# Both down projections as seven block products instead of eight

## The reference, cut to what matters

```python
# block 1 (D_FF = 2816)
h = rmsnorm(x, norm_ffn[layer])
x = x + (jax.nn.silu(h @ w_gate[layer]) * (h @ w_up[layer])) @ w_down[layer]
# block 2 (D_FF_2 = 4096)
h = _rmsnorm(x, mlp_norm_w[layer])
x = x + jnp.square(jax.nn.relu(h @ w_up[layer])) @ w_down[layer]
```

## Time and profile before

| | us |
|---|---|
| median of 3 runs (lowest to highest) | 3092.11 (3091.37 to 3097.47) |
| the profiled execution, first to last instruction | 3087.7 |
| TensorE busy | 2937.6 (95%) |
| VectorE busy | 1751.3 (57%) |
| ScalarE busy | 1204.6 (39%) |
| GpSimd busy | 1203.0 (39%) |
| mean granted TensorE clock | 0.986 |

### The profile page before, as it was taken

How to read it: one execution, slowest core, us unless ns; L and a number is a source line. 1 busy time by engine, 2 the same in 40 slices (tenths; PEclk the granted TensorE clock), 3 DMA queues, 4 the chain that set the end, 5 groups by cost and what they waited for, 6 DMA issues and landing times. The chain is left out here.

```text
span 3087.7 us, 36537 instructions
## 1 busy us (share of the span) xinstructions
PE 2937.6 (95%) x13886; PEld 2267.0 (73%) x13886; DVE 1751.3 (57%) x2645; ACT 1204.6 (39%) x1806; POOL 1203.0 (39%) x686
## 2 busy tenths in 40 slices
PE   7888998999999999999999899998999999999999
PEld 5656666666788788887887666656778788878887
DVE  5777775875232644445467555577552544455554
ACT  4445553555433433333124344456562322221110
POOL 5322334222244887774124101031103887722221
PEclk9999998999999999999999999999999999999999
DMA  7311212111251223334231311010003233342222
GB/s 199 71 49 48 62 49 55 42 56 55 85 188 48 68 83 86 84 86 137 67 102 43 114 34 38 17 41 18 11 4 109 83 109 109 109 163 95 95 75 75
DMA packets 279422, 236.36 MB, mean 77 GB/s; under 512 B 23860, under 2 KB 252084, under 8 KB 278708
## 3 DMA queue, kind: packets, MB, share of 16 engines
q1 hardware_dynamic: 279288, 234.65, 25.5%
HBM read 171.14 MB, written 53.51 MB: 73 GB/s over the span
## 5 line engine op out<-in xcount | busy, mean ns | idle before, releaser
L952 PE MATMUL big<-g_hi,w_hi 128*128 128x512 f32 x2112 | 688.5, 407 | 32.0 <-POOL w_lo L2458 6.7
L2458 POOL TENSOR_TENSOR w_lo<-w_raw,w_hi 128x1024 fp32r<-128x1024 f32 (+2 forms) x147 | 340.7, 2318 | 919.1 <-ACT w_hi L1375 919.1
L952 PE MATMUL big<-g_lo,w_hi 128*128 128x512 f32 x2112 | 660.0, 394 | 0.0
L952 PE MATMUL big<-g_hi,w_lo 128*128 128x512 f32 x2112 | 658.4, 393 | 0.0
L952 PEld LDWEIGHTS big<-g_hi,w_hi 128*128 128x128 f32 x2112 | 377.8, 190 | 191.2 <-issue 112.7
L952 PEld LDWEIGHTS big<-g_hi,w_lo 128*128 128x128 f32 x2112 | 399.7, 189 | 87.8
L952 PEld LDWEIGHTS big<-g_lo,w_hi 128*128 128x128 f32 x2112 | 398.9, 189 | 86.8
L1375 ACT ACTIVATE w_hi<-w_raw 128x1024 fp32r<-128x1024 f32 (+2 forms) x147 | 146.2, 995 | 417.1 <-PE big L952 402.7
L1403 ACT ACTIVATE a_hi<-a_raw 128x512 fp32r<-128x512 f32 x114 | 72.1, 632 | 332.9 <-POOL a_raw L2465 329.9
L1223 PE MATMUL big<-b_hi,a_hi 128*128 128x512 f32 x456 | 178.7, 392 | 7.9 <-DVE b_lo L2254 6.0
L1223 PE MATMUL big<-b_lo,a_hi 128*128 128x512 f32 x456 | 178.1, 391 | 0.0
(11 more groups left out here) (345 smaller groups left out, 5439.9 us busy)
## 6 DMA issues: line engine op xcount, KB each, us to landing
a_spill<-c SPq DMA_DIRECT2D x54, 512.0 KB, 3.4
g_lo<-a_spill SPq DMA_DIRECT2D x54, 512.0 KB, 5.1
w_raw<-in_w_in SPq DMA_DIRECT2D x51, 512.0 KB, 4.2
w_raw<-in_w_down SPq DMA_DIRECT2D x40, 512.0 KB, 4.3
w_raw<-in_w_up SPq DMA_DIRECT2D x27, 512.0 KB, 6.0
u_raw<-in_w_up SPq DMA_DIRECT2D x27, 512.0 KB, 5.9
rot<-rope_in SPq DMA_DIRECT2D x68, 128.0 KB, 2.3
g_spill<-gst_b SPq DMA_DIRECT2D x16, 512.0 KB, 3.0
```

Source lines behind the costliest of these rows:

```text
L952: ins = pe.matmul(out[0:m, HALF * h:HALF * h + HALF], w[slot][:, col:col + m], x[:, HALF * h:HALF * h + HALF], start=p == 0, stop=p == tot ...
L2458: pool.tensor_tensor(w_lo[s][:, 0:n], w_raw[s][:, 0:n], w_hi[s][:, 0:n].bitcast(F32), ALU.subtract).then_inc(*s_wlo.mark(w))
```

## The change

The down stage now uses the scheme of the up stage. The contraction runs over sets of two chunks (11 sets in mlp1, 16 in mlp2), the output over four jobs of two rows of `xres` each. For each set and job there are seven products of 3 matmuls instead of eight. The activation blocks of a set (two as they are, five differences and copies, 7 x 512 columns) are made in the up stage by VectorE (`even_difference`, `odd_differences`), stored in DRAM (`op_spill`) and come back set by set into four buffers. The weight sums are made by GpSimd (`down_weights`), from raw weights in stretches of one to three sets.

A window is a job with a stretch of sets: the seven products run over the stretch in PSUM, one bank each, and then VectorE adds every product into all the places of the rows where it belongs. There are 18 windows in mlp1, their widths in sets being 1 1 2 3 3 3 3 3 3 3 3 3 3 3 1 1 3 2, and 24 in mlp2: 1 1 2 3, then sixteen of 3, then 1 2 3 3. Two sets of four banks alternate. The norm factor moves into `form`. In mlp2 the square is now an instruction of its own on ScalarE (`square_act`). The job's stores are now of both tiles and the differences, and the next copy into `c1` still waits for the last of them (in mlp1 only every second time).

A cut of the diff:

```diff
--- before.py
+++ after.py
...
+    JOBS, WIDE = 4, 3
+    FINISH = {"mlp1": (0, 3, 1, 2), "mlp2": (2, 1, 0, 3)}
+    PARTS = [(0, 2), (2, 4), (4, 7)]
...
+    BANK_OF = (0, 1, 3, 0, 1, 2, 3)
+    ADDED_BEFORE = {3: 0, 4: 1, 6: 2}
+    ALSO = {0: 3, 1: 4, 2: 6}
+    BANK_FREE = {0: 3, 1: 4, 2: 6, 5: 5}
...
+    def windows(stage):
+
+        since, out = [0] * JOBS, []
+        for t in range(n_sets(stage)):
+            last = t == n_sets(stage) - 1
+            for job in FINISH[stage] if last else [job for job in (0, 3, 1, 2) if job % 3 == t % 3]:
+                out.append((job, since[job], t + 1, t))
+                since[job] = t + 1
+        return out
+
...
+    def bank_set(stage, i):
+
+        n = len(windows(stage))
+        if i < n - 2:
+            return i % 2
+        return n - 1 - i if stage == "mlp1" else 1
...
+                def down_product(i, pos):
+
+                    _, s0, s1, _ = plan[i]
+                    slot, g = d_slot(stage, i, pos), part_of(pos)
+                    out, n, at_set = bank_tiles[bank_set(stage, i)][BANK_OF[pos]], pos - PARTS[g][0], s1 - 1
+                    pe.wait_ge(*s_dlo.at(stage, i, pos))
+                    pe.wait_ge(*s_setl.at(stage, at_set, g))
+                    if pos in ADDED_BEFORE:
+                        pe.wait_ge(*s_drd.at(stage, i, ADDED_BEFORE[pos]))
+                    elif bank_before(stage, i) is not None:
+                        pe.wait_ge(*s_drd.at(stage, bank_before(stage, i), BANK_FREE[pos]))
+                    elif bank_set(stage, i):
+                        pe.wait_ge(*s_dr.at(stage, NJ - 1, "c21"))
+                    elif pos < 2:
+                        pe.wait_ge(*s_ar.at(stage, NJ - 1, pos))
+                    else:
+                        pe.wait_ge(*s_dr.at(stage, NJ - 1, "p3" if pos == 2 else "c11"))
+                    for k in range(s1 - s0):
+                        b = (s0 + k) % 4
+                        for z, (w, x) in enumerate(((d_hi, set_h), (d_hi, set_l), (d_lo, set_h))):
+                            ins = pe.matmul(out, w[slot][:, k, :], x[b][g][:, n, :], start=k == 0 and z == 0,
+                                            stop=k == s1 - s0 - 1 and z == 2)
+                    ins.then_inc(*s_dp.mark(stage, i, pos))
...
+                def square_act(m, r):
+
+                    act.wait_ge(*s_fn.at(stage, m, r))
+                    act.activation(crow[r][:, :], crow[r][:, :], ACT.Square).then_inc(*s_si.mark(stage, m, r))
...
+                    act.activation(set_h[b][g][:, :, :], set_z[b][g][:, :, :], ACT.Copy).then_inc(*s_seth.mark(stage, at_set, g))
...
+                        if not one:
+                            square_act(m - 1, 1)
...
+                        act.wait_ge(*s_fn.at(stage, m - 1, 1))
+                        if not one or m % 2 == 0:
+                            act.wait_ge(*s_asp[(m - 1) % 2].at(stage, m - 1))
...
+                    if not one:
+                        ins = dve.scalar_tensor_tensor(out=c, in0=c, scalar=0.0, in1=r_rep[:, :], op0=ALU.max, op1=ALU.mult)
+                    elif r == 0:
+                        ins = dve.tensor_tensor(c, c, r_rep[:, :], ALU.mult)
+                    else:
+                        dve.tensor_tensor(c, c, r_rep[:, :], ALU.mult).then_inc(*s_fn.mark(stage, m, "scaled"))
+                        dve.wait_ge(*s_fn.at(stage, m, "scaled"))
...
+                def even_difference(m, row):
+
+                    dve.wait_ge(*(s_fn.at(stage, m, 1) if one else s_si.at(stage, m, 0)))
+                    differ(row[:, HALF:T], row[:, HALF:T], row[:, 0:HALF], m, "even")
+
+                def odd_differences(m, even_row, t24_, t3):
+
+                    dve.wait_ge(*(s_fn.at(stage, m, 1) if one else s_si.at(stage, m, 1)))
+                    dve.wait_ge(*s_tf.at(stage, m - 1 if one else m, "even"))
+                    differ(t24_[:, 0:HALF], crow[1][:, HALF:T], even_row[:, HALF:T], m, "t2")
+                    dve.wait_ge(*s_tf.at(stage, m, "t2"))
+                    differ(t24_[:, HALF:T], crow[1][:, 0:HALF], t24_[:, 0:HALF], m, "t4")
+                    differ(t3, even_row[:, 0:HALF], t24_[:, 0:HALF], m, "odd")
...
-                        form(m, 0)
+                    form(m, 0)
                     if final:
-                        for k in range(2, 4):
-                            act_lo(0, k)
+                        for g in range(3):
+                            set_lo(0, g)
+                    if not one:
+                        even_difference(m, crow[0])
                     add(m, "u3", c21, c21, 6, at_("p3"))
...
+                for i, (job, s0, s1, t) in enumerate(plan):
+                    ra, rb = job_rows(stage, job)
+                    u, z = d_u[job][:, :], xres[:, rb, HALF:T]
+                    dest = [u, z, z, xres[:, ra, 0:HALF], xres[:, ra, HALF:T], u, xres[:, rb, 0:HALF]]
...
+                    for pos in range(7):
+                        dve.wait_ge(*s_dp.at(stage, i, pos))
+                        if pos in (2, 5, 6):
+                            dve.wait_ge(*s_drd.at(stage, i, {2: 1, 5: 0, 6: 2}[pos]))
+                        if pos == 0 and s0 == 0:
+                            dve.tensor_copy(dest[pos], banks_[BANK_OF[pos]]).then_inc(*s_drd.mark(stage, i, pos, "first"))
+                        else:
+                            dve.tensor_tensor(dest[pos], dest[pos], banks_[BANK_OF[pos]], ALU.add).then_inc(
...
+                        if pos in ALSO:
+                            both = dest[ALSO[pos]]
+                            dve.tensor_tensor(both, both, banks_[BANK_OF[pos]], ALU.add).then_inc(*s_drd.mark(stage, i, pos))
...
+                        if loading is not None and pos in (3, 4, 5):
+                            set_lo(loading, pos - 3)
+                        if one and leaving and pos in (2, 6):
+                            exit_row(job_rows(stage, plan[i - 1][0])[pos // 6])
+                        if ends_job(stage, i) and pos == 5:
+                            dve.wait_ge(*s_drd.at(stage, i, 5))
+                            dve.tensor_tensor(dest[4], dest[4], u, ALU.add).then_inc(*s_rel.mark(stage, ra))
+                            dve.tensor_tensor(z, z, u, ALU.add).then_inc(*s_du.mark(stage, job))
+                        if ends_job(stage, i) and pos == 6:
+                            dve.wait_ge(*s_drd.at(stage, i, 6))
+                            dve.tensor_tensor(dest[6], dest[6], u, ALU.add).then_inc(*s_rel.mark(stage, rb))
...
+                def down_weights(i, leaving_row=None):
+
+                    n = plan[i][2] - plan[i][1]
+                    block = lambda q: d_block(i, n, q)
+                    sums = lambda pos: d_sum[d_slot(stage, i, pos)][:, 0:n, :]
+                    down_sum(i, 1, block("A21"), block(A22), ALU.add, s_draw[i % 2].at(stage, i), *d_slot_free(stage, i, 1))
+                    down_sum(i, 5, sums(1), block(A11), ALU.subtract, s_dsum.at(stage, i, 1), *([s_dlo.at(stage, i - 1, 5)] if i else []))
+                    down_lo(i, 0)
+                    down_lo(i, 1, s_dsum.at(stage, i, 5))
+                    down_sum(i, 2, block("A21"), block(A11), ALU.subtract, *d_slot_free(stage, i, 2))
+                    down_lo(i, 2, s_dsum.at(stage, i, 2))
+                    down_lo(i, 3)
+                    if leaving_row is not None:
+                        add_squares("final", leaving_row)
+                    down_sum(i, 4, block(A12), d_s2[:, 0:n, :], ALU.subtract, *d_slot_free(stage, i, 4))
+                    down_lo(i, 4, s_dsum.at(stage, i, 4))
+                    down_lo(i, 5)
+                    down_lo(i, 6)
...
+                    out, done = op_spill[n // 2 if one else n], s_asp[n % 2]
+                    last = n == NJ - 1
+                    t24 = end_t24 if last else op_t24[stage]
+                    if not one:
+                        sp.wait_ge(*s_tf.at(stage, n, "even"))
+                        sp.dma_start(out[:, 0:2 * HALF], crow[0][:, :]).then_inc(*done.mark(stage, n, by=16))
...
+                    sp.wait_ge(*s_tf.at(stage, n, "odd"))
+                    t3 = crow[0] if one else (end_t3 if last else op_even[stage])
+                    sp.dma_start(out[:, 2 * HALF:3 * HALF], t3[:, 0:HALF]).then_inc(*done.mark(stage, n, by=16))
+                    sp.dma_start(out[:, 5 * HALF:7 * HALF], t24[:, :]).then_inc(*done.mark(stage, n, by=16))
...
```

More of the change, by code:

```diff
@@ new lines, in _emit, with d_slot_free, ends_job @@
+    D_ORDER = (A11, S1, S3, A12, S4, S2, A22)
+    LAST_ACT = 5
+    def d_slot_free(stage, i, pos):
+        NJ = n_jobs(stage)
+        if i == 0:
+            done = s_st.base(stage) + 7 * (NJ - 1)
+            return [s_al.at(stage, NJ - 1, S3)] if pos == 4 else [(s_st.sem, done + max(pos, 4))]
+        late = [s_tf.at(stage, "end"), s_asp[(NJ - 1) % 2].at(stage, NJ - 1)] if first_late(stage, i, pos) else []
+        return [s_dp.at(stage, i - 1, pos)] + late
+    def ends_job(stage, i):
```

(47 more changed lines are left out.)

682 lines of the change are left out of this document (239 added, 443 removed).

## The result

The changed kernel takes 3140.64 us (median of four, 3135.22 to 3142.37) where the kernel before takes 3091.74 (3085.65 to 3097.47): 1.0155 of it, 95% interval 1.0138 to 1.0172, so 1.6% slower. I had said 3128, in 3060 to 3160, and slower with 0.61. The profiled execution has a span of 3138.8 us against 3087.7.

The account below looks back on a forecast made before the run. TensorE was taken to bound the kernel at 0.2267 us a matmul. Terms -73.4 + 10.7 + 65.7 + 25.1 + 7.5 = +35.6 us took the span from 3087.7 to 3123.3, the median to 3128, range 3060 to 3160 (forecast's own 3100 to 3160).

Parts of the forecast that it names:

- mlp2's up stage, +65.7: From mlp2's up stage into its down stage's start: a 23.1 us loop replaces TensorE's 19.04 per job, costing +65.7 us.
- The turns: VectorE and GpSimd alternate on SBUF while GpSimd has work queued; in mlp2's up-stage loop 4.6 to 5.8 us, mean 5.2.
- my 17.9: mlp2's up-stage loop from copy to copy into `c1`, steps alone without waiting for GpSimd: 17.9 us.
- short turns: Rival: VectorE waits only for the GpSimd instruction already running; mlp2's loop about 20.6 us, total 3085; chance 0.2.
- hidden loop: Rival: mlp2's loop at 19.3 us or less never makes TensorE wait for `c1`; total 3058; chance 0.2.
- Middle windows, 0: Middle of both down stages: TensorE stays the bound, barely, at 14.3 us for a window of three sets; 0 us lost.
- a sign of being wrong: Stated in advance: the forecast is wrong if the down stages' middle windows are longer than 14.3 us.
- 57 of 57.2: GpSimd's load over four middle windows: 44 us of its own plus 13 lost to VectorE, against 57.2 available.
- Start of a down stage, +10.7: First two windows of mlp1's down stage: late VectorE, with set 0's lo parts ahead, loses 13.0 us against 2.3; +10.7.
- Where rows leave mlp1, +25.1: Last four windows of mlp1's down stage: VectorE's adds, sums and rows, with turns, take 73.0 us, 30.2 lost; +25.1.
- Where rows leave mlp2, +7.5: Last four windows of mlp2 to the end: 66.8 us, 24.0 over the matmuls against 16.5 now; +7.5.
- Between the down stage of mlp1 and the up stage of mlp2, 0: From `dv0` to mlp2's up stage: the forecast had no term for this stretch, counted as 0 us.

Follow-up runs that it names:

- e1: Changed kernel with mlp2's copy into `c1` waiting only for the two c rows' stores and the second difference; 3090.76 us against 3090.49 before the change, ratio 1.0000.
- e2: Changed kernel with GpSimd's 11 weight instructions per job in mlp2's up stage cut to 32 of 512 columns, leaving work out; span 3088.6 us against 3138.8.
- e3: Changed kernel with VectorE's four differences per job in mlp2's up stage cut to 32 columns, leaving work out; span 3110.5 us against 3138.8.
- e11: e1 with GpSimd adding the squares of rows that leave mlp1 in 32 of 1024 columns, leaving work out; span 3071.6 us, 7.6 below e1.

## Why the prediction held, and where it did not

- **mlp2's up stage, +65.7.** Right in mechanism, shown by e1: the loop through ScalarE, VectorE and the last store takes TensorE's place. The turns are 5.0 us of it (the relu instructions 0.95 and 0.6 longer than in e2, three differences 1.1, 1.0 and 1.0, c22 0.4), for my mean of 5.2. What is left is 17.3 for my 17.9: from the last difference to the copy, for one, it is 4.15 and not 4.4. The loop was 22.3 for my 23.1, 11 us less in 14 jobs, and its two ends took 4 us of that back. The rivals of short turns (20.6) and of a hidden loop (19.3) did not come. With the turns gone (e2) it is hidden, as my 17.9 had it.
- **The turns themselves.** Shown three ways: e2 takes them from VectorE, e3 leaves them when VectorE's instruction shrinks to 32 columns, e11 takes them away at mlp1's exit.
- **Middle windows, 0.** This step failed, by a sign of being wrong that I had named myself: windows longer than 14.3. It measures +10.0 and +12.0. I had put "57 of 57.2" for GpSimd over four windows and took that as "TensorE stays the bound, barely". The sum was the right thing to look at, and two of its terms were mis-sized. The 11 for GpSimd's 11 instructions left out that GpSimd also waits for ScalarE, 0.64 us at a time, to make the hi part of a sum that GpSimd has only just finished: a round without VectorE's lo parts takes 12.2, which is 4.8 more in four windows. VectorE's lo parts cost GpSimd 3.5 in each of three windows, 10.5 and not 13. So it is 59.3 of 57.2. That makes 7.5 of mlp2's 12.0; the other 4.5 fall in windows 3 to 5, at the start and with the last job's rest. The last job's product and differences, 6.0 of mlp1's 10.0, I had put in no window at all.
- **Start of a down stage, +10.7.** +8.9 in mlp1, the term was near. That the lo parts of set 0 ahead of the last sums cost it was only partly borne out: moved, they gave 1.1 in mlp1's first window, not the 2.2 expected, and none in mlp2.
- **Where rows leave mlp1, +25.1.** The same mechanism (e11), over-sized: 27.2 lost for my 30.2, and 7.3 were lost before where I had 5.1.
- **Where rows leave mlp2, +7.5.** +3.7. I ran no experiment on it.
- **Between the down stage of mlp1 and the up stage of mlp2, 0.** +10.6 that no step of mine had. From `dv0`'s last part to mlp2's first product it is 705.0 before and 715.6 in the changed kernel. The changed instructions alone do not force it: e1_early_copy has the same ones there and takes 704.2, e11_squares 705.1. But the nine other executions with the change have 708.1 to 713.3, and the one of e1_early_copy is its fastest of eleven by 6 us, so whether the change makes the longer ones likelier stays open. The granted clock goes with it (before, changed, e1_early_copy):

```profile
1750.00:2370.00 620.00, 584.24 (x2676) 422.24 (x2675) 359.38 (x629) 315.47 (x466) 105.33 (x43) 1.00 0.11 33
```
```profile
1750.00:2370.00 620.00, 584.52 (x2630) 419.35 (x2629) 362.49 (x634) 313.40 (x464) 96.15 (x39) 0.98 0.11 32
```
```profile
1750.00:2370.00 620.00, 582.98 (x2664) 418.34 (x2663) 365.05 (x637) 314.96 (x467) 100.53 (x41) 1.00 0.11 32
```

- **The total.** The 0s that failed are 34.0 us (22.0, 10.6 and the 1.4 ahead of mlp1, where the executions with the change differ by 6.6 among themselves), the four over-sized terms 18.1. The difference of 15.9 less the rounding of 0.4 is the 15.5 by which the span exceeds the 3123.3 forecast; the median is 12.6 over, inside the forecast's own range. The largest term was right in kind and near in size, but that the total came this close is in part luck: errors of both signs cancelled.
